# Turning the gated tile of five feed-forwards with VectorE and SBUF transfers instead of TensorE

## What is computed

```python
def swiglu(n, w_gate, w_up, w_down):
    return (jax.nn.silu(n @ w_gate) * (n @ w_up)) @ w_down
```

## Time and profile before

| | us |
|---|---|
| median of three runs | 1377.54 |
| lowest and highest of them | 1376.6, 1378.23 |
| the profiled execution | 1376.84 |
| its span | 1375.1 |

### The profile page before, as it was taken

How to read it: one execution, slowest core, us unless ns; L and a number is a source line. 1 busy time by engine, 2 the same in 40 slices (tenths; PEclk the granted TensorE clock), 3 DMA queues, 4 the chain that set the end, 5 groups by cost and what they waited for, 6 DMA issues and landing times.

```text
span 1375.1 us, 19419 instructions
## 1 busy us (share of the span) xinstructions
PE 1366.6 (99%) x6466; PEld 1135.6 (83%) x6466; DVE 853.6 (62%) x1350; ACT 774.4 (56%) x1251; POOL 50.0 (4%) x86
## 2 busy tenths in 40 slices
PE   9999999999999999999999999999999999999999
PEld 7888888888888888888888888888888888888887
DVE  6655556767655557755556676555566756665553
ACT  6555556645655546655556675555566675655552
POOL 1000010000000001000001010000002000000000
PEclk9999999999999999999999999999999999999999
DMA  8766626665666654766663347666455654575560
GB/s 292 233 205 218 214 92 203 214 202 169 199 200 204 191 176 138 229 195 189 190 198 100 120 134 240 204 190 186 152 144 179 201 169 138 168 230 183 185 209 33
DMA packets 198292, 251.57 MB, mean 183 GB/s; under 512 B 17922, under 2 KB 136928, under 8 KB 198240
## 3 DMA queue, kind: packets, MB, share of 16 engines
q1 hardware_dynamic: 197968, 250.86, 57.9%
q0 software_dynamic: 224, 0.03, 0.0%
q10 hardware_dynamic: 48, 0.02, 0.0%
HBM read 249.80 MB, written 1.05 MB: 182 GB/s over the span
## 4 chain that ended last, share of the span: by engine, by line
PE 95%; DVE 2%; ACT 1%; issue 1%; DMA 0%; SPq 0%; POOL 0%; DVEq 0%; ACTq 0%
PE ps L1933 30%; PE ps L1935 30%; PE ps L1934 29%; PE ps L1959 2%; PE ps L2072 2%; DMA raw<-in_ffn_w_up 0%; PE ps L2236 0%; PE ps L2588 0%; PE ps L2416 0%; PE ps L2417 0%; ACT whi L610 0%; DVE wlo L1226 0%; PE ps L2263 0%; POOL stat L586 0%; SPq L334 0%
## 5 line engine op out<-in xcount | busy, mean ns | idle before, releaser
L1223 DVE SCALAR_TENSOR_TENSOR wlo<-raw,gcol,whi 128x512 fp32r<-128x512 f32 x592 | 413.8, 746 | 274.0 <-ACT whi L610 273.9
L1933 PE MATMUL ps<-whi,kthi 128*128 128x512 f32 (+2 forms) x1384 | 548.4, 396 | 1.4 <-DVE wlo L1223 1.1
L1935 PE MATMUL ps<-whi,ktlo 128*128 128x512 f32 (+2 forms) x1384 | 537.1, 388 | 0.0
L1934 PE MATMUL ps<-wlo,kthi 128*128 128x512 f32 (+2 forms) x1384 | 536.3, 388 | 0.0
L610 ACT ACTIVATE whi<-raw,gcol 128x512 fp32r<-128x512 f32 x592 | 392.2, 714 | 228.5 <-PE ps L1935 223.2
L1935 PEld LDWEIGHTS ps<-whi,ktlo 128*128 128x128 f32 x1384 | 259.8, 188 | 54.3
L1933 PEld LDWEIGHTS ps<-whi,kthi 128*128 128x128 f32 x1384 | 260.0, 188 | 54.0 <-issue 1.9
L1934 PEld LDWEIGHTS ps<-wlo,kthi 128*128 128x128 f32 x1384 | 260.3, 188 | 48.9
L1231 DVE TENSOR_TENSOR wlo<-raw,whi 128x1024 fp32r<-128x1024 f32 x140 | 169.9, 1223 | 108.7 <-ACT whi L614 108.3
L614 ACT CAST whi<-raw 128x1024 fp32r<-128x1024 f32 x140 | 145.5, 1050 | 129.8 <-PE ps L1935 129.8
L1933 PE MATMUL ps<-whi,hthi 128*128 128x512 f32 x400 | 156.0, 390 | 0.0
(11 more groups left out here) (243 smaller groups left out, 807.2 us busy)
## 6 DMA issues: line engine op xcount, KB each, us to landing
raw<-in_ffn_w_gate SPq DMA_DIRECT2D x176, 256.0 KB, 2.9
raw<-in_ffn_w_up SPq DMA_DIRECT2D x176, 256.0 KB, 3.1
raw<-in_ffn_w_down SPq DMA_DIRECT2D x160, 256.0 KB, 3.4
raw<-in_w_in SPq DMA_DIRECT2D x80, 256.0 KB, 3.4
raw<-in_gmlp_w_in SPq DMA_DIRECT2D x64, 256.0 KB, 3.2
raw<-in_w_gate SPq DMA_DIRECT2D x44, 256.0 KB, 2.8
raw<-in_w_up SPq DMA_DIRECT2D x44, 256.0 KB, 3.1
raw<-in_w_down SPq DMA_DIRECT2D x40, 256.0 KB, 3.3
```

The costliest lines, as they stand in the source:

```text
L1223: ins = nc.vector.scalar_tensor_tensor(out=wlo[:, s, cut], in0=raw[:, s, cut], scalar=gcol[:, k:k + 1], in1=f32(whi[:, s, cut]), op0=ALU.m ...
L1933: nc.tensor.matmul(dst, lhs[0], rhs[0], start=first, stop=False)
L1934: nc.tensor.matmul(dst, lhs[0], rhs[1], start=False, stop=False)
L1935: return nc.tensor.matmul(dst, lhs[1], rhs[0], start=False, stop=last)
```

## The change

The 10 turns of each feed-forward that `hid_flip` did (tiles 0 to 9) are done without PE. DVE transposes `hid` in blocks of 32x32 into `hid_blocks` (`hid_turn`, two instructions a tile, one for each half of the tokens). That leaves each block in the wrong place: the transposed block of partition group i and column group j stands on partition group i and belongs on group j. SP moves the blocks with 16 transfers of 32 partitions by 128 columns (16 KB) from `hid_blocks` to `hid_moved`, both in `sq_out` in SBUF. They stand in SP's loop between slots 2 and 3. ACT and DVE then make `hthi` and `htlo` from `hid_moved` in SBUF. PE waits for the gated tile where it used to turn it.

The forget gates are made with the gate weights (16 and 8 columns) as the stationary operand and 256 tokens moving, 16 matmuls in place of 32; the result has gates on partitions, so ACT copies it to SBUF and PE turns it with two narrow transposes in `mix2_tile(3)`. The work of ACT and DVE on it is moved accordingly.

```diff
+            def hid_moves(n):
+
+                sp.wait_ge(sem("hid_turned"), n)
+                for i in range(4):
+                    for j in range(4):
+                        sp.dma_start(hid_moved[32 * j:32 * j + 32, i * P:(i + 1) * P],
+                                     hid_blocks[32 * i:32 * i + 32, j * P:(j + 1) * P]).then_inc(sem(f"hid_moved{i}"), 16)
...
-                        for s in range(4):
+                        for s in range(3):
                             gate_up(s, j + ahead[s], gate, up, j * FT + FT)
+                        hid_moves(j + ffns[0] * (NF - 1))
+                        gate_up(3, j + ahead[3], gate, up, j * FT + FT)
...
+                hid_moves(ffns[0] * (NF - 1))
                 if following:
                     following()
...
                 def turned_hidden(j):
 
-                    act.wait_ge(sem("hid_full"), j + (b + 1))
-                    nc.scalar.copy(hthi[:].rearrange("p c n -> p (c n)"), ps[:, 6, :]).then_inc(sem("ht_high"), 1)
+                    for i in range(4):
+                        act.wait_ge(sem(f"hid_moved{i}"), j * 64 + (moved * 64 + 64))
+                    nc.scalar.copy(hthi[:].rearrange("p c (t i x) -> p (c t) i x", t=2, i=4),
+                                   hid_moved.rearrange("p (i ct x) -> p ct i x", i=4, ct=4)).then_inc(sem("ht_high"), 1)
...
+            def hid_turn(n):
+
+                dve.wait_ge(sem("hid_ready"), n)
+                for t in range(TT):
+                    out = hid_blocks.rearrange("p (j c t x) -> p t c j x", j=4, c=2, t=2)[:, t]
+                    ins = nc.vector.transpose(out, hid[:, t, :].rearrange("p (c j x) -> p c j x", c=2, j=4))
+                ins.then_inc(sem("hid_turned"), 1)
...
                     for t in range(TT):
                         gated_tile(t, pre, j * 2 + (b + t + 1))
+                    hid_turn(j * 2 + (b + 2))
                     low(3, j + base[3], name)
...
                 with pe.Fori(2, NF - 1) as j:
+                    pe.wait_ge(sem("hid_ready"), j * 2 + b)
                     tile_product(lambda s: j + base[s])
                     down(j - 1)
-                    hid_flip(j)
...
-            def forget_gates(c, t):
...
+            def forget_gates(c):
+                nc.tensor.matmul(ps[0:16, 0, 0:S], f_high_low[:, c, :], kthi[:, c, :], start=c == 0, stop=False)
+                ins = nc.tensor.matmul(ps[0:8, 0, 0:S], f_high_low[:, c, 0:8], ktlo[:, c, :], start=False, stop=c == KC - 1)
+                if c == KC - 1:
+                    ins.then_inc(slot_used[4], 1)
+
+            def turn_gates():
+                pe.wait_ge(sem("f_read"), 1)
+                for t in range(TT):
+                    ins = nc.tensor.transpose(ps[:, 1, 16 * t:16 * t + 16], f_t[:, t * P:(t + 1) * P], ident[0:16, 0:16])
+                ins.then_inc(sem("f_turned"), 1)
```

More of the change, by code:

```diff
@@ L1061, in _ @@
             for n in range(1, 4):
-                for s in range(3):
+                for s in range(2):
                     more(s)
+                if n == 3:
+                    act.wait_ge(sem("f_turned"), 1)
+                    for t in range(TT):
+                        ins = nc.scalar.activation(st("f16", 32)[:, 16 * t:16 * t + 16], ps[:, 1, 16 * t:16 * t + 16], ACT.Copy,
+                                                   scale=st(f"r_pre_mix2{t}"))
+                    ins.then_inc(sem("f_ready"), 1)
+                more(2)
                 if n == 3:
@@ L1069, in _ @@
                 act.wait_ge(*latest(3))
+                if n == 2:
+                    act.wait_ge(*f_done)
+                    nc.scalar.copy(f_t, ps[0:16, 0, 0:S]).then_inc(sem("f_read"), 1)
                 if n == 3:
@@ L1080, in _ @@
                     more(3)
[L1081 to L1086, removed]
             for r in range(2):
@@ L1265, in turned_hidden @@
                     dve.wait_ge(sem("ht_high"), j + (b_ht + 1))
-                    nc.vector.tensor_tensor(htlo[:].rearrange("p c n -> p (c n)"), ps[:, 6, :],
-                                            f32(hthi[:]).rearrange("p c n -> p (c n)"), ALU.subtract
+                    nc.vector.tensor_tensor(htlo[:].rearrange("p c (t i x) -> p (c t) i x", t=2, i=4),
+                                            hid_moved.rearrange("p (i ct x) -> p ct i x", i=4, ct=4),
+                                            f32(hthi[:]).rearrange("p c (t i x) -> p (c t) i x", t=2, i=4), ALU.subtract
                                             ).then_inc(sem("ht_low"), 1)
@@ L1596, in _ @@
                 gated_tile(t, "pre_kv", count("silu_done"))
+            hid_turn(seen["silu_done"])
             more(1)
@@ L1724, in _, with fox_squares @@
             lows([0, 1, 2, 3], "mix2")
+            def fox_squares(qk, name):
+                dve.wait_ge(sem("mix_read"), 6 + 2 * qk)
+                nc.vector.tensor_reduce(st("s_" + name).rearrange("p (t h) -> p t h", t=TT),
+                                        fg[:, :, qk * 512:qk * 512 + 512].rearrange("p t (h r) -> p t h r", h=H),
+                                        AX_X, ALU.add).then_inc(sem("sum_ready"), 1)
+            lows([0, 1], "mix2")
             dve.wait_ge(sem("f_ready"), 1)
+            mark(nc.vector.memset(cum4, 0.0))
             dve.wait_ge(sem("bfor_in"), 16)
@@ L1979, in flip_h, with tile_product @@
                 flip(t, lambda c, t: h[:, t, c * P:(c + 1) * P], ready=renewed)
-            def tile_product(n_of, bank=4, between=None, beside=None):
+            def tile_product(n_of, bank=4, between=None, beside=None, at=3):
                 for s in range(4):
                     made(s, n_of(s))
-                    if s == 3 and between:
+                    if s == at and between:
                         between()
@@ L2147, in last_half @@
                     return ins
+                pe.wait_ge(sem("hid_ready"), b + 2 * last)
                 gate_up(last, 0).then_inc(sem("tile0_done"), 1)
@@ L2464, in _, with mix2_tile @@
                 take(s)
-            def mix2_tile(n, beside=None):
+            def mix2_tile(n, beside=None, between=None):
                 if n >= 2:
                     pe.wait_ge(sem("mix_read"), 2 * (n - 1))
-                tile_product(lambda s: use[s], bank=MIX2_BANK[n], beside=beside)
+                tile_product(lambda s: use[s], bank=MIX2_BANK[n], beside=beside, between=between, at=2)
                 for s in range(4):
@@ L2491, in _ @@
             made(4, take(4))
-            def forget_gates(c, t):
-                narrow = ps[:, t, 0:8], ktlo[:, c, t * P:t * P + P], f_high_low[:, c, 0:8]
-                both = ps[:, t, 0:16], kthi[:, c, t * P:t * P + P], f_high_low[:, c, :]
-                if c == 0:
-                    nc.tensor.matmul(*both, start=True, stop=False)
-                    nc.tensor.matmul(*narrow, start=False, stop=False)
-                else:
-                    nc.tensor.matmul(*narrow, start=False, stop=False)
-                    ins = nc.tensor.matmul(*both, start=False, stop=c == KC - 1)
-                    if c == KC - 1 and t == TT - 1:
-                        ins.then_inc(slot_used[4], 1)
+            def forget_gates(c):
[5 more added lines that the diff above has]
+                pe.wait_ge(sem("f_read"), 1)
+                for t in range(TT):
+                    ins = nc.tensor.transpose(ps[:, 1, 16 * t:16 * t + 16], f_t[:, t * P:(t + 1) * P], ident[0:16, 0:16])
+                ins.then_inc(sem("f_turned"), 1)
             mix2_tile(2, forget_gates)
-            mix2_tile(3)
+            mix2_tile(3, between=turn_gates)
             pe.wait_ge(sem("r_rotated"), 1)
```

34 lines of the change are left out of this document (13 added, 21 removed).

## The result

The changed kernel takes 1538.93 us in the median of four runs (1538.09 to 1539.88), the kernel before 1377.26 us beside it (1376.6 to 1378.23). The ratio is 1.117 (95% interval 1.115 to 1.119): the changed kernel is 162 us slower. The forecast was 1445, with a range up to 1540. Direction and range held, the size did not: +68 was forecast.

A forecast was written before the change was run, and what follows sets the result against it. PE, 99% busy, bounded the kernel; a 17.4 us loop would replace it. Four feed-forwards and the third's start and end gave 54.8 + 14.9 - 1.6 = +68 on 1376.84, so 1445 us; range 1375 to 1540.

The forecast's parts named there:

- the pitch of the 16 issues: SP's 16 transfers in a tile: issues 0.50 us apart, bounds 0.38 and 0.65, so 15 pitches take 7.5 us.
- Rival 2: SP's 16 issues: dear, pitch 0.65 as on fewer than 128 partitions, +112 us, 1557; chance 0.12.
- start: Start of each feed-forward: PE waits for tile 0's `htlo`, and tile 2 needs tile 1 gated; +2.1 us.
- tiles to the last pass: Eight more tiles in each feed-forward, each 0.6 us longer because the loop sets them; +4.8 us.
- wait for `htlo` at the end: End of each feed-forward: PE finishes the last tile's first half, then waits uncovered for `htlo`; +6.4 us.
- extra casts: End of each feed-forward: ACT's and DVE's casts of extra down rows follow `hthi`, delaying the last tile's first half; +0.4 us.
- A closed loop through SP, ACT and DVE sets the tile, not PE: From one DVE turn to the next: 17.4 us a tile, against 16.36 for PE alone and 16.80 before.
- The other terms: Rest of the loop: landing 2.1 us, `hthi` to next weight 0.6, on to the gated tile 6.3, wait and transposes 0.8.
- rival 3: Landing of the last move: late, 3.4 us as for the down rows, +65 us, 1510; chance 0.08.
- rival 1: SP's 16 issues: cheap, faster below a pitch of about 0.415; 1364 at 0.38, 1353 at its limit; chance 0.13.
- The third feed-forward worse by 1.2 than the others: Third feed-forward: SP issues tile 2's first slots late, so its start costs +3.3 us and the whole 14.9.
- The forget gates: Gate matmuls: 16 narrow pairs at 0.24 us replaced by 16 matmuls and two transposes; net -1.6 us, bounds 0 and -3.

The follow-up runs named there:

- experiment 7: The changed kernel with its 16 transfers in another form in each feed-forward (source, partitions, row size), placing nothing rightly; run once, 1516.31 us.
- experiments 2 and 3: The changed kernel with only 12, then only 8, of the 16 transfers a tile, the rest left stale; 1412.92 us and 1356.85 us.
- experiment 3: The changed kernel with 8 of the 16 transfers a tile, so half of each turned tile is stale; 1356.85 us, ratio 0.986.
- experiment 9: The changed kernel with 28 small matmuls into an unused PSUM bank in the wait at each feed-forward's end; 1532.14 us, ratio 1.112.
- experiment 4: The changed kernel with `turned_hidden` of the tile before put behind slot 1 in ACT's and DVE's programs, all 16 transfers kept; 1475.82 us, ratio 1.072.
- experiment 1: The kernel before with only the forget gates changed, feed-forwards as before; 1376.24 us, ratio 0.9995.

## Why the prediction was right in kind and wrong in size

The term that failed is "I take 0.50, near the rows of like form": the pitch of the 16 issues. It measured 0.63. At the prediction's own 750 us for each microsecond of pitch that is +98, and the total was short by 94. The rows that I chose from the earlier trace rows all had DRAM at one end, and experiment 7 shows that a move between two SBUF places is 0.17 dearer than the same move from DRAM, and that the size and number of rows don't change it. Rival 2 had the right size (0.65) for the wrong reason: it laid the high pitch of the earlier trace rows to fewer partitions, which makes no difference (0.64 on 128), and those transfers came from DRAM as well. My bounds held the value; within them I went by the form of the transfer, and not by where its ends lie.

Put in place, term by term, with the fourth feed-forward from the gating of tile 0 (925.02 after, 825.79 before) to PE's turn in the last tile (1113.75 after, 983.60 before), +30.9 in all:

| step | forecast | measured | where |
|---|---|---|---|
| start | +2.1 | +4.0 | tile 2 may begin 19.31 after tile 0 was gated (when tile 1 is gated) instead of 15.35 (when PE has turned it, 841.14); SP begins its moves only at 926.29, 0.46 after DVE's turn, since loads of slot 2 stand before them |
| tiles to the last pass | +4.8 | +17.0 | eight of 18.84, and 0.7 more (tile 9 gated at 1095.76) |
| wait for `htlo` at the end | +6.4 | +7.7 | 7.67 idle |
| clock after it | 0 | +1.8 | 4.46 instead of 2.72 |
| extra casts | +0.4 | 0 | gated at 1112.24, before PE's turn |

The measured terms sum to 30.5 of 30.9. The lags by feed-forward were 34.4, 32.2, 32.6, 31.0 and 32.5. Their sum, 162.7, less the gates' 1.4 is 161.3, and the spans differ by 161.2.

- *A closed loop through SP, ACT and DVE sets the tile, not PE:* right. 18.84 where PE's own work is 16.36; experiments 2 and 3 move it by what they take out.
- *The other terms:* landing 1.8 for 2.1, transposes 0.77 for the 0.76 that a pair of other SBUF operations of that size had, weights and gates 6.22 for 6.3, `hthi` to weight 0.52 for 0.6. Together they made the loop 0.5 shorter than forecast, the issues 1.9 longer.
- *The Trainium skill's 50 ns.* DMA: Bandwidth & Descriptors, section Anatomy of one DMA, gives the sequencer some 50 ns, but in an account of transfers that GpSimd issues, which the prediction set beside SP's without saying so. Here 800 issues by SP have a median of 0.59 us, twelve times that, so the figure doesn't carry over to them. The same section's total of about 2.0 us is near the 1.8 from issue to landing.
- *Late landing (rival 3):* not so. *Cheap issues (rival 1):* not so; by its own rule eight issues make the tile PE's own and the sign turns, as experiment 3 shows.
- *Five waits of some 6 us at the ends:* right, 6.2 to 8.4; but that a wait has a second price, the clock, was missing. At the five ends it is 10.2 us of the 162, and experiment 9 got 6.8 of it back.
- *The third feed-forward worse by 1.2 than the others:* not seen, its lag of 32.6 is like the others'.
- *Missing altogether:* that SP's program with 28 issues takes 17.3 to 17.7 us in most tiles by itself, more than PE's 16.36. The chain hid it. Had the loop been opened first, the change would still lose (experiment 4).
- *The forget gates:* right, -1.4 in the span for -1.6 (-0.9 in the medians of experiment 1).

## What to carry to other kernels

Price each transfer of a chain by its issue, and take the price from a row whose two ends lie in the same memories; sixteen small ones in one queue were 9.4 us that no bandwidth figure shows, and also 10 us of the queue's own time a tile, which must fit beside its loads. A detour off the busiest engine pays only where its whole latency is covered: here the eight middle turns could go (18 us faster), while the first and the last of each feed-forward had to stay. Where TensorE is made to wait, add what its clock loses afterwards.

## What the runs showed of the hardware

- An issue from SBUF to SBUF took 0.59 us (pitch 0.63) for 32, 64 or 128 partitions and rows of 128 to 512 B; from DRAM to SBUF 0.42 (0.463) for the same 16 KB; one of 256 KB from SBUF to DRAM 0.34. Two other kinds of load from DRAM took 0.57 to 0.67.
- Two queues issued such transfers at the same time, with a pitch of 0.63 on SP, as alone, and 0.64 on ACT.
- Behind weight loads, a write of 256 KB to DRAM landed 4.9 us after its issue (median of 50), and four reads of it took SP 1.76.
- After TensorE had stood 7.67 us its matmuls came 0.43 apart, and 0.23 only from the ninth on; after 6.4 us of small matmuls and 1.17 of rest they came at 0.23 at once. At other places a wait of 2.27 was followed by the slow pace too (at 1071.50), and one of 2.20 by the fast one (at 976.67), so the wait's length alone doesn't tell.
